# Half-length inverse transforms, attention levels in 64-token blocks, and log decays in another order, in a two-layer hybrid encoder

## The reference

```python
def gla_group(...):      # 4 heads, DK = 64, DV = 128, forward and backward
    S_t = diag(exp(g_t)) S_{t-1} + k_t^T v_t ;  o_t = q_t S_t      # g = log_sigmoid(z) / 16
    o = rmsnorm(o_forward + o_backward) * silu(r)

def fft_long_conv(u, k_freq, d):                # u: (B, 256, 512)
    return irfft(rfft(u, n=512) * k_freq, n=512)[:, :256] + u * d

def hyena_group(...):
    z = x1 * fft_long_conv(v, k_freq[:, 0], skip[0])
    z = x2 * fft_long_conv(z, k_freq[:, 1], skip[1])
    return rmsnorm(z, norm_w)

x = x + concat(gla, hyena) @ w_out ;  x = x + swiglu(rmsnorm(x))
```

## Time and profile before

| | |
|---|---|
| median of 3 runs | 1446.55 us (1445.41 to 1447.95) |
| the profiled execution | 1445.8 us |
| its span, first to last instruction | 1444.0 us |
| mean granted clock | 0.995 |
| PE busy, share of the span | 1396.2 us, 97% |
| DVE / ACT / POOL busy | 457.1 / 484.4 / 688.1 us |

### The profile page before, as it was taken

How to read it: one execution, slowest core, us unless ns; L and a number is a source line. 1 busy time by engine, 2 the same in 40 slices (tenths; PEclk the granted TensorE clock), 3 DMA queues, 4 the chain that set the end, 5 groups by cost and what they waited for, 6 DMA issues and landing times.

```text
span 1444.0 us, 16910 instructions
## 1 busy us (share of the span) xinstructions
PE 1396.2 (97%) x7056; PEld 1114.4 (77%) x7056; DVE 457.1 (32%) x673; ACT 484.4 (34%) x733; POOL 688.1 (48%) x423
## 2 busy tenths in 40 slices
PE   6799999999999999999999999999999999999997
PEld 5567777788888778888876777777888888888885
DVE  5745864533202310000054677554240000000003
ACT  5834323333323222212147533322343223222112
POOL 2534554345455544554422765633635555554431
PEclk9899999999999999999999999999999999999999
DMA  6211111113333322333221212111223333333332
GB/s 251 72 31 44 44 45 59 44 50 97 103 97 100 88 88 88 106 98 102 88 65 52 74 45 59 59 30 44 82 65 102 89 102 102 88 114 105 88 101 74
DMA packets 31179, 116.85 MB, mean 81 GB/s; under 512 B 3456, under 2 KB 3584, under 8 KB 30720
## 3 DMA queue, kind: packets, MB, share of 16 engines
q1 hardware_dynamic: 31104, 115.78, 26.3%
HBM read 113.67 MB, written 2.10 MB: 80 GB/s over the span
## 4 chain that ended last, share of the span: by engine, by line
PE 86%; DVE 9%; ACT 2%; issue 1%; POOL 1%; DMA 1%; POOLq 0%; DVEq 0%; SPq 0%; ACTq 0%
PE ps L1052 16%; PE ps L1054 16%; PE ps L1053 15%; PE ps L1060 7%; PE ps L1063 7%; PE ps L1061 7%; PE ps L1261 4%; PE ps L1247 3%; PE ps L1183 2%; PE ps L1128 2%; PE ps L1082 2%; DVE amat L897 2%; DVE ring L881 1%; PE ps L1208 1%; PE ps L1115 1%
## 5 line engine op out<-in xcount | busy, mean ns | idle before, releaser
L663 POOL TENSOR_TENSOR w_lo<-w_raw,w_hi 128x1024 fp32r<-128x1024 f32 x192 | 460.4, 2398 | 504.9 <-ACT w_hi L403 504.9
L1052 PE MATMUL ps<-h_hi,w_hi 128*128 128x512 f32 (+1 forms) x1064 | 433.1, 407 | 1.3 <-POOL w_lo L663 1.3
L1054 PE MATMUL ps<-h_hi,w_lo 128*128 128x512 f32 (+1 forms) x1064 | 413.9, 389 | 0.0
L1053 PE MATMUL ps<-h_lo,w_hi 128*128 128x512 f32 (+1 forms) x1064 | 413.4, 389 | 0.0
L403 ACT ACTIVATE w_hi<-w_raw 128x1024 fp32r<-128x1024 f32 x192 | 201.6, 1051 | 204.0 <-PE ps L1063 200.3
L1052 PEld LDWEIGHTS ps<-h_hi,w_hi 128*128 128x128 f32 x1064 | 200.4, 188 | 50.6 <-issue 8.2
L1053 PEld LDWEIGHTS ps<-h_lo,w_hi 128*128 128x128 f32 x1064 | 200.6, 189 | 46.4 <-issue 7.2
L1054 PEld LDWEIGHTS ps<-h_hi,w_lo 128*128 128x128 f32 x1064 | 200.3, 188 | 42.1
L1026 DVE TENSOR_TENSOR hid<-ps,sg 128x512 f32<-128x512 f32 x44 | 30.4, 692 | 429.0 <-PE ps L1054 429.0
L1060 PE MATMUL ps<-w_hi,hid_hi 128*128 128x512 f32 x352 | 139.3, 396 | 1.8 <-POOL w_lo L663 1.8
L1061 PE MATMUL ps<-w_lo,hid_hi 128*128 128x512 f32 x352 | 138.8, 394 | 0.0
(11 more groups left out here) (151 smaller groups left out, 1627.1 us busy)
## 6 DMA issues: line engine op xcount, KB each, us to landing
w_raw<-in_units SPq DMA_DIRECT2D x198, 512.0 KB, 3.6
par<-in_par SPq DMA_DIRECT2D x2, 1310.5 KB, 8.8
gain<-in_gain SPq DMA_DIRECT2D x5, 512.0 KB, 4.6
x<-in_x SPq DMA_DIRECT2D x4, 512.0 KB, 6.7
out_y<-x SPq DMA_DIRECT2D x4, 512.0 KB, 2.6
cst<-in_cst SPq DMA_DIRECT2D x1, 1536.0 KB, 15.7
mask_f<-in_mask SPq DMA_DIRECT2D x1, 640.0 KB, 12.5
cst<-in_cst SPq DMA_DIRECT2D x1, 224.0 KB, 3.8
```

What stands on the lines that cost most here:

```text
L663: nc.gpsimd.tensor_tensor(w_tile(g, 1), w_raw[:, g % RAW], w_tile(g, 0).bitcast(F32), ALU.subtract).then_inc(s_lo, 1)
L1052: nc.tensor.matmul(out, hi, act_hi, start=start, stop=False)
L1053: nc.tensor.matmul(out, hi, act_lo, start=False, stop=False)
L1054: return nc.tensor.matmul(out, lo, act_hi, start=False, stop=stop)
```

## The change

1. **Inverse transforms.** The second half of the frequencies is ordered backwards, so that its basis functions equal the first half's on even tokens and are opposite on odd tokens. VectorE adds and subtracts the two halves ("folds", four operations per pair), and `back` does two matmuls of 128 columns for the even and two for the odd tokens in place of four of 256. `gating` reads and writes with a step of two tokens. The two sums of `products` move from GpSimd to VectorE.
2. **Levels in blocks of 64.** Levels 3 to 7 and the product of `g1` and `g2` are computed only in 64 x 64 blocks on the diagonal, two levels to a PSUM bank. The masked copies go into a tile `near` (128 x 256), and ScalarE copies it into `amat` (`near_copy`) before `attend`. Puts no longer stand between steps 2 and 3.
3. **Log decays.** Ln directly behind Exp; the q and k copies on VectorE; the two `bt` copies on ScalarE (`shift_sums`); the scans of the heads in slots 2, 4 and 5; the first level step waits for `zmin`; `exponents` ahead of `lo_unit` on GpSimd; the second sine in slot 3.

```diff
+            def shift_sums(L, h):
+
+                act.wait_ge(scan.sem, scan.at(L, h + 1))
+                b, c = (t[:, h].rearrange("p (s t) -> p s t", s=NSEQ) for t in (bt, cum))
+                nc.scalar.activation(b[0:DK], c[0:DK], ACT.Copy)
+                nc.scalar.activation(b[DK:P, :, 1:SEQ], c[DK:P, :, 0:SEQ - 1], ACT.Copy).then_inc(btd.sem, 1)
+
             def evacuate(L, t):
+                kind, i = KINDS[t]
+                if kind in ("q", "k"):
+                    return
...
                     c = BRANCH[kind] + i
+                    if kind == "hv":
+
+                        act.wait_ge(scan.sem, scan.at(L, HEADS))
...
             def big_levels(L, h):
                 act.wait_ge(pair.sem, pair.at(L, 4 * h + 2))
                 a = acs.next()
-                nc.scalar.activation(amat[:, 0].rearrange("p s j i -> p (s j i)"), ps[:, LA, :], ACT.Copy)\
-                    .then_inc(acs.sem, 1)
+                tiles = amat[:, 0].rearrange("p s j i -> p (s j) i")
+                forward, backward = (ps[:, LA + way, :].rearrange("p (l n c) -> p l n c", l=2, n=TT) for way in range(2))
+                nc.scalar.activation(near, forward[:, 0], ACT.Copy).then_inc(acs.sem, 1)
+                nc.scalar.activation(tiles[0:BLOCK, :, BLOCK:P], forward[0:BLOCK, 1], ACT.Copy)
+                nc.scalar.activation(tiles[BLOCK:P, :, 0:BLOCK], backward[BLOCK:P, 1], ACT.Copy)
                 act.wait_ge(acs.sem, a)
-                bw = ps[:, LA + 1, :].rearrange("p (s j i) -> p s j i", s=NSEQ, j=2)
-                for rows, cols in ((slice(64, P), slice(0, 64)), (slice(32, 64), slice(0, 32)),
-                                   (slice(96, P), slice(64, 96))):
-                    last = nc.scalar.activation(amat[rows, 0, :, :, cols], bw[rows, :, :, cols], ACT.Copy)
+                for rows in (slice(32, 64), slice(96, P)):
+                    last = nc.scalar.activation(near[rows, :, 0:32], backward[rows, 0, :, 0:32], ACT.Copy)
                 last.then_inc(big.sem, 1)
+
+            def near_copy(L, h):
+                act.wait_ge(put.sem, put.at(L, 10 * h + 10))
+                tiles = amat[:, 0].rearrange("p s j i -> p (s j) i")
+                for e in range(2):
+                    rows = slice(BLOCK * e, BLOCK * e + BLOCK)
+                    last = nc.scalar.activation(tiles[rows, :, rows], near[rows], ACT.Copy)
+                last.then_inc(nearc.sem, 1)
...
-                    if L == 0 and slot == 4:
-                        sine_of(L, 1, hid_a, P)
...
                     if slot == 1:
-                        a = gate_logs(L)
+                        gate_logs(L)
+                    if slot in (2, 3):
+                        shift_sums(L, slot - 2)
+                    if L == 0 and slot == 3:
+                        sine_of(L, 1, hid_a, P)
+                    if slot in (6, 7):
+                        shift_sums(L, slot - 4)
                     if L == 0 and (slot, 0) in S_AT[L]:
                         filter_copy(L, *S_AT[L][slot, 0])
+                    for h in range(HEADS):
+                        if slot == 4 * h + 8:
+                            near_copy(L, h)
                     evacuate(L, slot)
                     if L and (slot, 1) in S_AT[L]:
...
-            def sums(L, n):
...
             for L in range(DEPTH):
                 for slot in range(U_OUT):
+                    exponents(L, slot)
                     lo_unit(L * UNITS + slot + 2)
-                    if (slot - 1, 1) in D_AT:
-                        sums(L, D_AT[slot - 1, 1])
-                    exponents(L, slot)
-                    if (slot, 0) in D_AT:
-                        sums(L, D_AT[slot, 0])
...
+            def gate_parts(L):
+                for h in range(HEADS):
+
+                    v.wait_ge(zabs.sem, zabs.at(L, h + 1))
+                    nc.vector.tensor_scalar(zneg[:, h], ps[:, 2 + h, :], par[:, C_BG + h:C_BG + h + 1], 0.0,
+                                            ALU.add, ALU.min).then_inc(zmin.sem, 1)
+
+                nc.vector.memset(bt.rearrange("p h (s t) -> p (h s) t", s=NSEQ)[DK:P, :, 0:1], 0.0)
+
+            def evacuate(L, t):
+
+                b = ps[:, t % 2, :]
+                v.wait_ge(s_unit, L * UNITS + t + 1)
+                kind, i = KINDS[t]
+                scale, fwd, bwd = (DK ** -0.5, g2, g1) if kind == "q" else (1.0, g1, g2)
+                for n in range(2):
+                    h = 2 * i + n
+                    rows = slice(DK * n, DK * n + DK)
+                    nc.vector.tensor_scalar(fwd[0:DK, h], b[rows], scale, None, ALU.mult)
+                    last = nc.vector.tensor_scalar(bwd[DK:P, h], b[rows], scale, None, ALU.mult)
+                last.then_inc(qk.sem, 1)
+
             def gate_sums(L, h):
-                v.wait_ge(zabs.sem, zabs.at(L, h + 1))
-                nc.vector.tensor_scalar(zneg[:, h], ps[:, 2 + h, :], par[:, C_BG + h:C_BG + h + 1], 0.0,
-                                        ALU.add, ALU.min).then_inc(zmin.sem, 1)
                 v.wait_ge(zln.sem, zln.at(L, h + 1))
...
-                v.wait_ge(scan.sem, scan.at(L, h + 1))
-                b, c = (t[:, h].rearrange("p (s t) -> p s t", s=NSEQ) for t in (bt, cum))
-                nc.vector.tensor_copy(b[0:DK], c[0:DK])
-                nc.vector.tensor_copy(b[DK:P, :, 1:SEQ], c[DK:P, :, 0:SEQ - 1]).then_inc(btd.sem, 1)
...
                         nc.vector.copy_predicated(
-                            amat[:, 0].rearrange("p s j i -> p (s j) i"),
-                            mask[:, l - 3, way].unsqueeze(1).to_broadcast([P, 4, P]),
-                            ps[:, (LC if l % 2 else LA) + way, :].rearrange("p (n c) -> p n c", n=4))\
+                            near, mask[:, l - 3, way].unsqueeze(1).to_broadcast([P, TT, BLOCK]),
+                            ps[:, level_bank(l) + way, level_cols(l)].rearrange("p (n c) -> p n c", n=TT))\
...
+                re, im = spec[:, 2 * d], spec[:, 2 * d + 1]
                 v.wait_ge(ufp.sem, ufp.at(L, n + 1))
                 if n:
                     v.wait_ge(yfd.sem, yfd.at(L, n))
-                nc.vector.tensor_tensor(spec[:, 2 * d], ur, kr, ALU.mult)
+                nc.vector.tensor_tensor(re, ur, kr, ALU.mult)
                 nc.vector.tensor_tensor(prod[:, 0], ui, ki, ALU.mult)
                 nc.vector.tensor_tensor(prod[:, 1], ur, ki, ALU.mult)
-                nc.vector.tensor_tensor(spec[:, 2 * d + 1], ui, kr, ALU.mult).then_inc(prd.sem, 1)
+                nc.vector.tensor_tensor(im, ui, kr, ALU.mult).then_inc(prd.sem, 1)
+                v.wait_ge(prd.sem, prd.at(L, n + 1))
+                nc.vector.tensor_tensor(re, re, prod[:, 0], ALU.subtract)
+                nc.vector.tensor_tensor(im, im, prod[:, 1], ALU.add).then_inc(yfd.sem, 1)
+                if d:
+
+                    v.wait_ge(yfd.sem, yfd.at(L, n + 1))
+                    for c in range(2):
+                        nc.vector.tensor_tensor(even_odd[0][c], spec[:, c], spec[:, 2 + c], ALU.add)
+                    for c in range(2):
+                        last = nc.vector.tensor_tensor(even_odd[1][c], spec[:, c], spec[:, 2 + c], ALU.subtract)
+                    last.then_inc(folded.sem, 1)
 
...
                 v.wait_ge(invp.sem, invp.at(L, n + 1))
                 z = u[:, 4 * (o + 1) + 2 * b:4 * (o + 1) + 2 * b + 2, SEQ * s:SEQ * s + SEQ]
-                nc.vector.tensor_tensor(z, ps[:, 6 + b, :].rearrange("p (c t) -> p c t", c=2), z, ALU.mult)\
+                z = z.rearrange("p c (t e) -> p c t e", e=2)
+                nc.vector.tensor_tensor(z, ps[:, 6 + b, :].rearrange("p (c e t) -> p c t e", c=2, e=2), z, ALU.mult)\
                     .then_inc(gated.sem, 1)
...
-                        for h in range(HEADS):
-                            gate_sums(L, h)
+                        gate_sums(L, 0)
+                    if KINDS[slot][0] in ("q", "k"):
+                        evacuate(L, slot)
+                    if slot in (2, 4, 5):
+                        gate_sums(L, max(1, slot - 2))
...
-                        pe.wait_ge(scan.sem, scan.at(L, HEADS))
+                        pe.wait_ge(zmin.sem, zmin.at(L, HEADS))
...
                     for n in range(TT):
-                        nc.tensor.matmul(ps[:, LA, P * n:P * n + P], g1[:, h, tok(n)], g2[:, h, tok(n)],
-                                         start=True, stop=True)
+                        for e in range(2):
+                            cols = slice(P * n + BLOCK * e, P * n + BLOCK * e + BLOCK)
+                            nc.tensor.matmul(ps[BLOCK * e:BLOCK * e + BLOCK, LA, BLOCK * n:BLOCK * n + BLOCK],
+                                             g1[:, h, cols], g2[:, h, cols], start=True, stop=True)
...
-                    pe.wait_ge(put.sem, put.at(L, 10 * h + (0, 0, 2, 6)[p]))
-                    pe.wait_ge(big.sem, big.at(L, h + 1))
+                    if p == 2:
+                        pe.wait_ge(big.sem, big.at(L, h + 1))
```

(34 more changed lines are left out.)

60 lines of the change are left out of this document (28 added, 32 removed).

## The result

The changed kernel takes 1428.32 us (median of 4 runs, 1427.74 to 1429.22) against 1447.22 for the kernel before (4 runs, 1445.41 to 1447.95). The ratio is 0.987, 95% interval 0.9858 to 0.9882: faster by 18.9 us (1.3%), where 52.6 was forecast. The profiled execution has a span of 1426.2 us, 17.8 less than before.

What follows compares the result with a forecast made beforehand. It took TensorE, busy 97% of 1444.0 us, as the bound: -47.9 work, -10.6 gate stage, +5.9 VectorE waits give -52.6, forecast 1394 us; 8 in 10 range 1385 to 1414.

Steps and rivals of the forecast that it cites:

- The saved work: TensorE in the mixers: inverse transforms 26.9 us, levels 17.6 and product of g1 and g2 3.4 less, 47.9 in all.
- VectorE in the mixer: Slots 11-12, 16, 19 and 22: later VectorE chains, in steps of 0.60, make TensorE wait 17 us against 11.1: +5.9.
- limit that the prediction named for being wrong: Forecast wrong if the waits at slots 12, 16, 19, 22 pass 30 us or small matmuls step over 30 ns.
- no clock dip: Sign in the new profile: no wait over 2 us at layer 0's first level step and no clock dip.
- The gate stage: Layer 0's log decays, copies and scans: the 9.2 us wait before the first level step goes, 10.6 us gained.
- about 1 us in slot 5: Layer 0: hidden_pair late behind the k copies and the third scan, about 1 us.
- the same edit gains nothing: Gate stage in layer 1: filter transforms fill these slots and no wait stands there, so no gain.
- The shared port: Rival: VectorE's SBUF operations slowed by the port pair shared with GpSimd, +18.7 us at eight places, 1413 us; chance 0.16.
- The gate wait stays: Rival: the gate chain through ScalarE's tables slips by a slot, gain only 42 us, 1405 us; chance 0.10.
- No new waits at all: Rival: no new TensorE waits, a gain of 58 us or more, 1386 us or less; chance 0.08.
- Issue binds: Rival: 1408 small matmuls keep a step of 62 ns, +44.2 us, 1459 us in all; chance 0.04.
- two tiles side by side: Rival: only two tiles run together, not four; levels and g gain nothing, 1412 us; chance 0.12.

Runs made afterwards that it cites:

- e1: The changed kernel plus 141 useless TensorE matmuls in the places where TensorE waits: 1414.91 us, ratio 0.9782.
- e7: The changed kernel with VectorE's gate-stage order and TensorE's order in slots 12, 16, 20 and 22 both changed, same work: 1395.18 us, ratio 0.9638.
- e12: e7 with the first two pairs of folds behind the puts and ScalarE's turn_copy ahead of its exponentials in slot 17: 1384.52 us, ratio 0.9567.
- e9: The changed kernel with GpSimd's w_lo subtraction cut from 1024 columns to 64 in units 3 to 24 of each layer: 1400.44 us, ratio 0.9679.
- e3: The changed kernel with the gate stage of before the change: 1424.54 us, ratio 0.985.
- e2: The kernel before with the inverse transforms' part of the change alone: 1454.73 us, ratio 1.0058.
- e11: e2 with TensorE's order in slots 12, 16, 20 and 22 changed: 1424.44 us, ratio 0.9843.

## Why the prediction was wrong

- **The saved work** was right. `back` was forecast at 1.78 us a call and takes 1.79; a masked level behind another at 14.5 ns an instruction, and takes 14.4; the product of `g1` and `g2` at 0.46, and takes 0.62, so that it saves 2.2 us and not 3.4. That four tiles run side by side holds. The rule of a floor of about 25 ns between starts, as the prediction cited it from the Trainium skill ("TensorE: Matmul & The Clock Gate", section "Wait — 56ns, not 53.3ns?"), does not hold for 64x64 tiles here: the measurement decides. A check over both mixers (layer 0 from 25 us on): the time without waits of over 0.15 us and without the loss at the lower clock (the estimate at e1) is 536.0 us before and 489.5 in the changed kernel, 46.6 less; in e7 it is 490.4, in e12 491.5. The 47.9 was right within 3.
- **The first step that failed** is "VectorE in the mixer", "each followed in layer 0 by steps of 0.60", with its sum of 17 us. The waits in slots 12 to 22 are 14.1 us in layer 0 and 14.2 in layer 1 where 8.5 was forecast for each. The steps of 0.60 held for the operations on PSUM, and not for those between SBUF tiles that met a long GpSimd operation. In slot 12 the wait is 4.3 and not 1.3, and the four folds alone took 6.1 us and not 2.4. In slot 20, which the list doesn't have, `back(4)` waits 2.1 for its folds, behind a sum of 2.89 us. In slot 22 `turn_o` waits twice, 1.8 and 2.1, first for VectorE's queue and then for one stretched scaling; the forecast had one wait of 2.6. Slots 16 (2.9 against 3.3) and 19 (0.8 against 1.3) were right. Neither limit that the prediction named for being wrong was passed: these waits sum to 28.3 us, under its 30, and the small matmuls step by 14.4 ns, under its 30. The mean of the sums and folds is 0.88 us, under its 1.0, so a mean doesn't show the trouble either. What did show it was the clock, where it had said "no clock dip".
- **The gate stage**: the wait of 9.2 went, as forecast, but "about 1 us in slot 5" was 4.6. These lines of VectorE show what `hidden_pair` stood behind:

```profile
60.77 2.28 DVE L900 TENSOR_TENSOR_SCAN cum<-v_tok,u 128x256 f32<-128x256 f32 x2
62.97 0.74 DVE L859 COPY hid_b<-hid_a 64x256 f32<-64x256 f32 x1
63.72 2.33 DVE L861 TENSOR_SCALAR hid_b<-hid_a 64x256 f32<-64x256 f32 x1
```

  and GpSimd's line beside the last of them:

```profile
63.52 2.38 POOL L694 TENSOR_TENSOR w_lo<-w_raw,w_hi 128x1024 fp32r<-128x1024 f32 x1
```

  In e9 the same two scans take 1.48 us and L861 0.83, together 2.3 less, and the wait is 2.2 less: about half of the 4.6 is stretching and the rest the queue. Layer 1, where "the same edit gains nothing", lost 3.5 us: the two scans of one head took 3.61 us there, ahead of six ring products. e3 shows the sum: -10.6 was forecast, and the new stage cost some 3 to 4 us more than the old one.
- **The second step that failed was a term put at nothing.** The prediction had read the lower clock behind the wait of 9.2 us and counted it as a gain when that wait went, but gave none of its own new waits of 2 to 4 us such a price. e1 measured it: at least 13.4 us, and some 19 by the estimate (20.7 less the 1.7 that e1 has left).
- **The account**, of the two traces (their spans differ by 17.8), with the clock as estimated:

| us | forecast | traces |
|---|---|---|
| TensorE's own work, mixers | -47.9 | -46.6 |
| waits of TensorE, mixers | -2.4 | +18.1 |
| loss at the lower clock, mixers | -2.3 | +17.8 |
| stages outside the mixers | 0 | -7.2 |
| sum | -52.6 | -17.9 |

  The forecast of the waits is -9.2 - 0.6 + 1.5 + 5.9, that of the clock the 1.8 + 0.5 of the gate stage. Each was some 20 us too low, and 7.2 us came from stages that the sum doesn't have. Without them the kernel would be only some 11 us faster. A shorter account, 52.6 less 20.3 for the waits and 13.4 for e1's clock, gives 18.9, just what the medians differ by. That match is luck: e1's 13.4 is a lower bound, and what it lacks is about what the other stages gave.
- **The rivals.** "The shared port" was the right mechanism at 0.16: its +18.7 us (1413) is near the 20.3 that came, but it spread them over its eight places, and they came in slots 12, 20 and 22 and in slot 5. It was priced for the waits alone; with the 13.4 of the clock it would have been 1426. Even so e9 and e12 show it as one of two conditions: without GpSimd's long operations 17 of the 40 us of waits are gone, and with another order 28. "The gate wait stays" was half right: it moved. "No new waits at all" (1386 or less) describes e12 (1384.5), though 7.2 us of e12's gain lie outside the mixers. "Issue binds" and "two tiles side by side" are ruled out by the durations of the chain.

What stays open: why the untouched stages are 7.2 us shorter, and the wait of 2.4 us in slot 5 of layer 1, which is left in e12.

## What to carry to other kernels

When TensorE's work shrinks in a kernel that it bounds, the engines beside it have less time for their own queues: follow each queue at its crowded places with the long durations of a line, not with its median, and shift TensorE's side steps by half a unit where a queue ends close. Each wait can have a second price in the matmuls beside and behind it, here at least 13.4 us and by estimate 20.7 for ten stretches of lower clock, against 40.3 of waits; read the clock by short windows, as the page's slices hide it. Compare the stages that a change doesn't touch as well: here they gave 7.2 of 17.8 us. A change that measures slower alone (e2, +0.6%) can be worth most of its work (e11) once the order around it is adapted, so try the reordering before dropping it.

## What the runs showed that was not expected

- Useless matmuls put into waits made a kernel 13.4 us faster, since they kept the clock at 2.4 GHz (e1).
- VectorE operations between SBUF tiles took 0.42 or 0.69 us alone and up to 2.6 or 2.9 us beside a GpSimd operation of 2.4 to 2.9 us, ending 0.28 to 0.55 us behind it; the products that read PSUM (L964 to L967) were never stretched. An operation with one input tile is stretched too: L861 took 2.33 us for 64x256 beside a `w_lo` of 2.38, where it took 0.83 in e9 beside shorter ones.
- 32 instructions in 64x64 tiles with 64 columns, four quarters in turn, step by 14.4 ns on the average.
- Stages with the same instructions and the same granted clock took 851.2 us in some kernels and 858.4 in others; no run shows why.
